# Regrouping the token-wise input products of a hybrid attention block: five groups of 512 columns in place of seven groups of 384 and 256

## The reference, cut to what matters

```python
def hybrid_layer(x, mem, norm_g, w_in, w_out, mem_norm_g, w_mem_kv, qk_g):
    h = rms_norm(x, norm_g)
    proj = jnp.einsum('btd,de->bte', h, w_in)
    ...
    a_q, a_k, a_v, a_g, b_q, b_k, b_v, b_g, m_q, m_g = jnp.split(proj, cuts, axis=-1)
    qa = rope(rms_norm(to_heads(a_q, N_HEADS_MOBA), qk_g[0]))
    ka = rope(rms_norm(to_heads(a_k, N_HEADS_MOBA), qk_g[1]))
    oa = from_heads(moba_attention(qa, ka, to_heads(a_v, N_HEADS_MOBA)))
    qb = rope(rms_norm(to_heads(b_q, N_HEADS_DIL), qk_g[2]))
    kb = rope(rms_norm(to_heads(b_k, N_HEADS_DIL), qk_g[3]))
    ob = from_heads(dilated_attention(qb, kb, to_heads(b_v, N_HEADS_DIL)))
    mkv = jnp.einsum('bmd,de->bme', rms_norm(mem, mem_norm_g), w_mem_kv)
    m_k, m_v = jnp.split(mkv, 2, axis=-1)
    qm = rms_norm(to_heads(m_q, N_HEADS_MEM), qk_g[4])
    km = rms_norm(to_heads(m_k, N_HEADS_MEM), qk_g[5])
    om = from_heads(memory_attention(qm, km, to_heads(m_v, N_HEADS_MEM)))
    y = jnp.concatenate([oa * jax.nn.silu(a_g), ob * jax.nn.silu(b_g), om * jax.nn.silu(m_g)], axis=-1)
    return x + jnp.einsum('bte,ed->btd', y, w_out)
```

## Time and profile before

| | us |
|---|---|
| median of three runs | 1634.05 |
| the three runs | 1631.53, 1634.05, 1634.16 |
| the profiled execution | 1631.64 |
| span of its profile | 1629.8 |
| PE busy | 1576.7 (97%) |
| DVE busy | 921.9 (57%) |
| ACT busy | 755.0 (46%) |

### The profile page before, as it was taken

One profiled execution on the slowest core, in us unless ns is written; L12 is line 12 of the kernel. 1 busy time (PEld: TensorE's weight loads), 2 busy tenths in 40 slices (PEclk: granted clock), 3 DMA queues, 4 the chain that ended last, 5 costly groups with the idle time before them and its releaser, 6 DMA issues.

```text
span 1629.8 us, 22039 instructions
## 1 busy us (share of the span) xinstructions
PE 1576.7 (97%) x8345; PEld 1305.3 (80%) x8345; DVE 921.9 (57%) x1940; ACT 755.0 (46%) x1587; POOL 46.4 (3%) x75
## 2 busy tenths in 40 slices
PE   6999999999998999999999999999999999999999
PEld 6887778788887887877788888899866779987677
DVE  4597546443444479656435335549665564885653
ACT  5443544333333362555323334535565654556662
POOL 0000001000001000000100000100000010000000
PEclk9999999999999999999999999999999999999999
DMA  7232112333332433212232333333211233312121
GB/s 220 88 90 78 52 40 78 91 93 101 90 101 62 121 91 95 61 52 68 65 103 80 103 102 118 93 88 85 60 47 56 66 107 98 98 51 63 40 78 65
DMA packets 80886, 136.07 MB, mean 83 GB/s; under 512 B 8191, under 2 KB 33549, under 8 KB 80781
## 3 DMA queue, kind: packets, MB, share of 16 engines
q1 hardware_dynamic: 77120, 129.22, 27.0%
q10 hardware_dynamic: 3660, 5.44, 1.1%
HBM read 132.55 MB, written 2.10 MB: 83 GB/s over the span
## 4 chain that ended last, share of the span: by engine, by line
PE 86%; DVE 9%; ACT 3%; issue 1%; DMA 0%; ACTq 0%; POOL 0%; DVEq 0%
PE gemm_bank L728 71%; PE aux_bank L854 3%; PE aux_bank L833 3%; PE aux_bank L814 2%; PE aux_bank L798 2%; DVE w_lo L1472 2%; PE aux_bank L783 1%; ACT w_hi L1107 1%; DVE rope L1574 1%; PE aux_bank L700 1%; PE aux_bank L1017 0%; PE aux_bank L842 0%; PE aux_bank L908 0%; DVE q L1535 0%; DVE k L1535 0%
## 5 line engine op out<-in xcount | busy, mean ns | idle before, releaser
L1107 ACT ACTIVATE w_hi<-raw 128x512 fp32r<-128x512 f32 (+3 forms) x524 | 305.2, 587 | 625.5 <-PE gemm_bank L728 624.9
L1472 DVE TENSOR_TENSOR w_lo<-raw,w_hi 128x512 fp32r<-128x512 f32 (+3 forms) x524 | 330.0, 635 | 427.2 <-ACT w_hi L1107 425.5
L728 PE MATMUL gemm_bank<-act_hi,w_hi 128*128 128x512 f32 x768 | 311.4, 405 | 9.4 <-DVE bgT L2085 3.3
L728 PE MATMUL gemm_bank<-act_hi,w_lo 128*128 128x512 f32 x768 | 300.1, 391 | 0.0
L728 PE MATMUL gemm_bank<-act_lo,w_hi 128*128 128x512 f32 x768 | 299.7, 390 | 0.0
L728 PE MATMUL gemm_bank<-w_hi,act_hi 128*128 128x384 f32 (+3 forms) x736 | 265.6, 361 | 1.1 <-DVE qk_c L1512 1.1
L728 PE MATMUL gemm_bank<-w_hi,act_lo 128*128 128x384 f32 (+3 forms) x736 | 256.9, 349 | 0.0
L728 PE MATMUL gemm_bank<-w_lo,act_hi 128*128 128x384 f32 (+3 forms) x736 | 256.7, 349 | 0.0
L728 PEld LDWEIGHTS gemm_bank<-act_hi,w_hi 128*128 128x128 f32 x768 | 144.2, 188 | 47.4 <-issue 15.3
L728 PEld LDWEIGHTS gemm_bank<-act_hi,w_lo 128*128 128x128 f32 x768 | 144.3, 188 | 31.1
L728 PEld LDWEIGHTS gemm_bank<-act_lo,w_hi 128*128 128x128 f32 x768 | 144.6, 188 | 28.6 <-issue 1.0
(11 more groups left out here) (303 smaller groups left out, 2093.9 us busy)
## 6 DMA issues: line engine op xcount, KB each, us to landing
raw<-in_w_in SPq DMA_DIRECT2D x104, 512.0 KB, 3.6
raw<-in_w_in SPq DMA_DIRECT2D x64, 384.0 KB, 3.3
raw<-in_w_out SPq DMA_DIRECT2D x32, 512.0 KB, 3.9
raw<-in_w_branch SPq DMA_DIRECT2D x24, 512.0 KB, 3.8
raw<-in_w_mem_kv SPq DMA_DIRECT2D x8, 512.0 KB, 3.7
raw<-in_w_in SPq DMA_DIRECT2D x16, 256.0 KB, 2.8
raw<-in_w_in SPq DMA_DIRECT2D x8, 416.0 KB, 4.8
x<-in_x SPq DMA_DIRECT2D x4, 512.0 KB, 5.1
```

Of the source, the lines that this page charges most:

```text
L728: last = pe.matmul(o, a, c, start=begin and n == 0, stop=end and n == 2)
L1107: act.activation(w_hi[:, s % RING, 0:n], raw[:, p % RAW, kk % PIECE, 0:n], ACT.Copy)\
L1472: dve.tensor_tensor(w_lo[:, s % RING, 0:n], raw[:, p % RAW, kk % PIECE, 0:n], w_hi[:, s % RING, 0:n].bitcast(F32), ALU.subtract).then_inc( ...
```

## The change

The seven token-wise products of a layer of block 2 are no longer groups of their own. Their 2560 columns stand in one line, aq, ak, bq, bk, av, bv, mq, and are cut every 512 columns: t0 is aq and the first 128 columns of ak, t1 the other 256 of ak and 256 of bq, t2 the last 128 of bq and bk, t3 is av and 128 of bv, t4 the other 256 of bv and mq. t0, t1, t2 are plain, t3 is led (in av's place), t4 is filler (in place of bv and mq). A weight piece of such a group is two DMAs, one for each part, and a bank is evicted in two instructions, all on ACT. The events ahead of the led group move two k-steps later, and scores 3 goes to the start of attention. The heads of a have three pieces for each k-step over t2 and the first three of t3, and those of b begin with k-step 5 of t3.

```diff
+TOKEN_FEATURES = [("aq", 0, WA), ("ak", WA, WA), ("bq", 4 * WA, WB), ("bk", 4 * WA + WB, WB),
+                  ("av", 2 * WA, WA), ("bv", 4 * WA + 2 * WB, WB), ("mq", 4 * WA + 4 * WB, WE)]
+def token_groups():
+    out, at = [[]], 0
+    for what, c0, n in TOKEN_FEATURES:
+        done = 0
+        while done < n:
+            if at == T:
+                out.append([])
+                at = 0
+            m = min(n - done, T - at)
+            out[-1].append((what, done, at, c0 + done, m))
+            at, done = at + m, done + m
+    return out
...
-        two("aq", 0, WA)
-        two("ak", WA, WA)
-        two("bq", 4 * WA, WB)
-        two("bk", 4 * WA + WB, WB)
-        two("av", 2 * WA, WA)
-        two("bv", 4 * WA + 2 * WB, WB)
-        two("mq", 4 * WA + 4 * WB, WE)
+        for tag, segments in TOKENS.items():
+            def tokens(k0, k1, segments=segments, l=l):
+                return [(at, w["w_in_2"][l, k0 * P:k1 * P, c:c + m]) for _, _, at, c, m in segments]
+            add((2, l, tag), tokens, KD, T, 4)
...
-        fill = [((2, l, g), KD) for g in ("bv", "mq", "ag", "bg", "mg")] + [((2, l, "out", 0), EARLY)]
+        fill = [((2, l, g), KD) for g in ("t4", "ag", "bg", "mg")] + [((2, l, "out", 0), EARLY)]
...
-        a.lead = {2: [("turn", 0, 0)], 3: [("low", 0, 0)], 4: [("scores", 0)], 5: [("scores", 2)], 6: [("scores", 3)]}
-        for m in (2, 3):
-            a.begin[0].remove(("scores", m))
+        a.lead = {4: [("turn", 0, 0)], 5: [("low", 0, 0)], 6: [("scores", 0)], 7: [("scores", 2)]}
+        a.begin[0].remove(("scores", 2))
...
-            evict(gi_of(2, l, "aq"), ACT.Copy, lambda b: flat_2("aq")[:, b, :])
-            split.through(gi_of(2, l, "ak"))
+            def evict_tokens(name):
+                gi = gi_of(2, l, name)
+                for b in range(NT):
+                    wait_gemm_full(act, gi, b)
+                    for what, c, at, _, m in TOKENS[name]:
+                        ins = act.activation(flat_2(what)[:, b, c:c + m], gemm_bank[b][:, at:at + m], ACT.Copy)
+                    ins.then_inc(gemm_read[b], 1)
+            for name in ("t0", "t1"):
+                split.through(gi_of(2, l, name))
+                evict_tokens(name)
...
-            gi = gi_of(2, l, "av")
+            gi = gi_of(2, l, "t3")
             for kk in range(KD):
-                for _ in range(2):
-                    next(b_squares, None)
+                if kk > 4:
+                    for _ in range(2):
+                        next(b_squares, None)
                 split.beside(gi, kk)
...
-            evict(gi_of(2, l, "ak"), lambda b: flat_2("ak")[:, b, :])
+            split.through(gi_of(2, l, "t1"))
...
-            alongside(a_heads, [gi_of(2, l, n) for n in ("bq", "bk")], 2)
+            alongside(a_heads, [gi_of(2, l, "t2")], 3, drain=False)
             for kk in range(KD):
                 for event in a.lead.get(kk, []):
                     if event[0] != "turn":
                         begin(a, *event)
-                for _ in range(2):
+                for _ in range(3 if kk < 3 else 0):
+                    next(a_heads, None)
+                for _ in a_heads if kk == 3 else ():
+                    pass
+                for _ in range(2 if kk > 4 else 0):
                     next(b_heads, None)
-                split.beside(gi_of(2, l, "av"), kk)
+                split.beside(gi_of(2, l, "t3"), kk)
```

More of the change, by code:

```diff
@@ L57 @@
 PIECE = 2
+TOKEN_FEATURES = [("aq", 0, WA), ("ak", WA, WA), ("bq", 4 * WA, WB), ("bk", 4 * WA + WB, WB),
[12 more added lines that the diff above has]
+    return out
+TOKENS = {f"t{i}": segments for i, segments in enumerate(token_groups())}
 def constants():
@@ L576, in mode @@
         def mode(self, key):
-            return "tokens" if key[2] in ("vc", "bv", "mq", "out") else "features"
+            return "tokens" if key[2] in ("vc", "out") or key[2] in TOKENS else "features"
         def step_that_ends(self, *key):
@@ L847, in values @@
             if a.block == 2 and g in (0, FIRST_B):
-                wait_gemm_read(pe, gi_of(2, a.l, "bv" if g else "av"))
+                wait_gemm_read(pe, gi_of(2, a.l, "t4" if g else "t3"))
             aux_wait_read(pe, a.key("T", a.steps_of[g * NT + NT - 1][-1]))
@@ L1383, in block_2 @@
         def block_2(l):
-            evict(gi_of(2, l, "aq"), ACT.Copy, lambda b: flat_2("aq")[:, b, :])
-            split.through(gi_of(2, l, "ak"))
+            def evict_tokens(name):
[8 more added lines that the diff above has]
+                evict_tokens(name)
             def kind_tiles(a):
                 return [kinds[a + n][:, t, :, :] for n in ("q", "k") for t in range(NT)]
-            wait_gemm_read(act, gi_of(2, l, "aq"))
-            wait_gemm_read(act, gi_of(2, l, "ak"))
+            wait_gemm_read(act, gi_of(2, l, "t1"))
             for n, _ in enumerate(head_squares(kind_tiles("a"), sq_2)):
[L1393 to L1397, removed]
+                split.beside(gi_of(2, l, "t2"), n // 2)
+            split.through(gi_of(2, l, "t2"))
+            evict_tokens("t2")
+            wait_gemm_read(act, gi_of(2, l, "t2"))
             b_squares = head_squares(kind_tiles("b"), sq_2)
             a = attention_2(l)
-            gi = gi_of(2, l, "av")
+            gi = gi_of(2, l, "t3")
             for kk in range(KD):
-                for _ in range(2):
-                    next(b_squares, None)
+                if kk > 4:
+                    for _ in range(2):
+                        next(b_squares, None)
                 split.beside(gi, kk)
@@ L1410, in block_2 @@
                         exponentials(a, event[1])
-            evict(gi, ACT.Copy, lambda b: flat_2("av")[:, b, :])
+            for event in a.lead[KD - 1]:
+                exponentials(a, event[1])
+            split.through(gi)
+            evict_tokens("t3")
             m_squares = head_squares([mq_tok[:, t, :, :] for t in range(NT)]
                                      + [mkv[:, t, 0, :, :] for t in range(NMEM // P)], sq_2)
-            n_m = a.step_that_ends(2, l, "mq")
+            n_m = a.step_that_ends(2, l, "t4")
             _, hi_at, _ = y2_plan(a)
@@ L2048, in block_2 @@
             dve.wait_ge(causal_loaded, 16)
-            split.through(gi_of(2, l, "aq"))
-            evict(gi_of(2, l, "ak"), lambda b: flat_2("ak")[:, b, :])
+            split.through(gi_of(2, l, "t0"))
+            split.through(gi_of(2, l, "t1"))
             def kind_heads(a, gain):
```

12 lines of the change are left out of this document (6 added, 6 removed).

## The result

The changed kernel takes 1653.43 us (median of four runs, 1651.03 to 1654.15), the kernel before 1634.11 in the same comparison (1631.53 to 1634.71): the ratio is 1.0119, with a 95% interval from 1.0101 to 1.0136, so 19.3 us or 1.2% slower. The forecast was 1649, in a range from 1638 to 1660.

A forecast was written before the change was run, and what follows sets the result against it. PE's own work, plus a few waits for DVE or ACT, was taken as the bound. A layer adds 14.5 and saves 6.45 us, +16.1 for two; from 1632.8 that gave 1649, range 1638 to 1660.

The forecast's parts named there:

- The waits that come: New PE waits for DVE or ACT in block 2, priced place by place: 14.5 us a layer.
- turn 0: PE reaches it after twelve k-steps of t2 and t3, before the heads of a end: 1.0 us a layer (0.3 to 2).
- scores 4: Attention scores waiting for low parts of pair 1, queued on DVE behind two sums: 1.9 us a layer (1.2 to 2.6).
- T(3): Step behind scores 4, waiting for exponentials whose row maxima follow a Newton chain on DVE: 1.5 us a layer (1.0 to 2.0).
- turn 3: Heads of b, only six pieces done ahead of attention, are drained there: the largest wait, 3.9 us a layer (3.3 to 4.4).
- The waits that go: Waits at scores 3, scores 7 and two old borders removed or shortened, with restarts: 3.9 us a layer (3.3 to 3.9).
- PE's saving: In block 2, 192 fewer matmuls a layer at 13.3 ns fixed part each, same columns: 2.55 us saved a layer.
- lesser shifts: Small added waits at scores 11, 19 and 23: 0.6 us a layer (0 to 1.2).
- The clock: Rival: new long waits lower PE's clock, adding 6 to 8 us in all, giving 1656; chance 0.11.
- a granted clock under 0.99: Sign in the changed profile that was to show the lower PE clock at work.
- Late pieces: Rival: narrower weight DMAs come late, 2.72 us for each piece missed, a few a layer giving 1660; chance 0.04.
- The faster rival: DVE and ACT run further ahead, most added waits fall, some −2 us a layer, 1629; chance 0.14.

The follow-up runs named there:

- experiment 6: The kernel of experiment 5 with the filler's banks shared out so four borders lie between steps, and a third piece of the heads of b at steps 2, 7, 9: 1615.52 us.
- experiment 9: The kernel before (seven groups) with low parts ahead of the weight splitting, and filler shared out so mq ends with step 10 and bg with step 28: 1619.01 us.
- experiment 10: The kernel before with each weight piece of its seven token-wise groups loaded by two DMAs instead of one: 1632.63 us.
- experiment 1: The changed kernel with three pieces of the heads of b instead of two at each attention step from step 2 on: 1648.49 us.
- experiment 2: The changed kernel with filler weights of six steps changed so borders ag/bg, bg/mg and mg/out0 lie between two steps: 1647.37 us.
- experiment 4: The kernel before (seven groups) with squares and heads of b begun at k-step 5 of av instead of k-step 0: 1642.05 us.
- experiment 3: The changed kernel with the squares and sums of b one k-step of the led group earlier (from k-step 4): 1640.79 us.
- experiment 5: The kernel of experiment 3 with a pair's low parts on DVE ahead of the splitting of weights of the turn's step: 1633.17 us.

## Why the prediction was right, point by point

**The waits that come** were taken place by place, and the distances from start to start, less columns and 13.3 ns, give them again (layer 0, layer 1; the last row is what the four waits grew by against the kernel before):

| place | forecast | measured |
|---|---|---|
| turn 0 | 1.0 | 1.14, 1.14 |
| turn 1 | 1.2 | 0.96, 0.95 |
| scores 4 | 1.9 | 1.93, 0.94 |
| T(3) | 1.5 | 1.43, 1.44 |
| turn 3 | 3.9 | 3.74, 3.74 |
| border of ag and bg | 2.3 | 2.25, 2.24 |
| border of mg and out0 | 2.1 | 1.98, 1.98 |
| scores 11, 15, 19, 23 | 0.6 | 0.7, 1.2 |

Turn 3 shows how such a term is reckoned. The timeline of layer 0:

```profile
1186.56 0.45 PE L833 MATMUL aux_bank<-k_hi,q_hi 64*128 64x384 f32 x2
...
1187.50 0.56 DVE L1663 CUSTOM_DVE_ANT_0 probs<-aux_bank,mask_square 128x384 f32<-128x384 f32 x1
...
1192.53 0.95 DVE L1611 TENSOR_TENSOR bk<-rope,rope 128x768 f32<-128x768 f32 x1
...
1193.59 1.12 PE L802 MATMUL aux_bank<-ident,bq 128*128 128x128 f32 x4 [3.53 <-DVEq L1616]
```

Scores 10 start at s = 1186.56, the row maximum at s+0.94, the last subtraction ends at s+6.92, the turn starts at s+7.03; forecast were s+0.93, s+6.95 and 0.2 more. Here the mechanism was forecast, and not only the number.

**The waits that go** came to 1.0, 1.13, 1.13 and 0.6, 3.87 a layer for 3.9. The borders that were to keep 0.4 and 1.2 keep 0.50 and 1.20. (The four terms of the text add up to 3.29 and not to 3.35, and a restart cost 0.16 to 0.21 and not 0.13; the two slips nearly cancel.)

**PE's saving** is seen in the matmuls, 384 fewer, whose 512 columns stand 227 ns apart as before. By the earlier trace rows they are worth 5.1 us. All of PE's distances in block 2 add up with it: in the two layers 2.56 and 2.55 less for the matmuls, 10.3 and 9.8 more of waits (idle for over 0.1 us), 1.4 and 3.5 more at low clock, and 0.2 more and 0.4 less of the rest make the 9.25 and 10.40. Experiments 6 and 9 lie 3.5 apart, with 0.7 of waits against the five groups. The Trainium skill (TensorE: Matmul & The Clock Gate, Back-to-back issue gap) has 2.5 ns as the fixed part of an isolated matmul's gap; by an estimate from that page five groups could be worth 1 us here. The measured 3.5 agrees with the rows and not with this estimate, as far as two versions that differ in more than their groups can tell.

**Where the sum was off.** It gave +16.1 and block 2 grew by 19.65. Without the clock it was 14.5: scores 4 were priced with a table load that ACT has in layer 0 only, 1 us too much in layer 1, and most other terms run up to 0.2 high (turn 0 is 0.1 low). In the "lesser shifts" 1.5 at scores 15 were not seen; they were made up for in part by scores 11, which wait less behind the long wait at turn 3 (0.7 and 0.2 less), and by scores 19 (0.2 less). The clock, +5.1, was in the text as a rival with 6 to 8 and a chance of 0.11: it did not stand in the forecast's place but came on top of it. A cost that follows from the forecast's own waits belonged in the sum as a term, not among the rivals. That the time came within 4.4 us of the forecast is thus in part luck: a term that was left out and waits that were priced too high stand against each other.

Two things on the clock were also read wrongly. The low stretch of the earlier trace rows does not follow the border of bg and mg, which PE reaches only at 1248.9; it follows scores 19:

```profile
1229.93 0.50 PE L814 MATMUL aux_bank<-k_hi,q_hi 64*128 64x512 f32 x2 [1.64 <-DVE k_lo L1620]
```

And a granted clock under 0.99 could not have been its sign: 6 to 8 us of 1650 lower the mean by no more than 0.005, and it went from 0.999 to 0.994. The rule of the Trainium skill (TensorE: Matmul & The Clock Gate, What's actually happening), 1.2 GHz after idleness and 2.4 GHz again with activity, agrees with the stretches at both turns 3 (0.55 to 0.60 granted). Layer 0's border of ag and bg, with the same wait of 2.25 as layer 1's, keeps full clock, and no run here shows why.

**What the rivals were worth.** Late pieces: no (experiment 10, and the `w_lo` waits beside it). The faster rival: no, `k_lo` of pair 1, which was to decide, came after PE (1.9 and 0.9 us). The rival of the experiments, that a wait which is taken away comes back at the next place, is half right: experiments 1 and 2 show waits that change places and 4 a wait that covers another, 3 and 5 show waits that go. What the evictions in two pieces, and that of ak on ACT, add to turn 0 (1.14 a layer) was not tested by itself.

## What to carry to other kernels

Fewer and wider groups save a fixed part for each matmul, but they move every border, event and piece of side work that is placed by count: price each of these by what then stands ahead of it on the engine that is waited for. Before work is moved to end a wait, look for idle time of that engine, and look at what is queued behind the place it is moved to: put into an idle stretch most of it was gained, put ahead of the next awaited instruction it was paid back. A long wait covers later ones, which come out when it goes. An instruction that others wait for should not stand behind one that waits itself: that order alone cost the kernel before 7.6 us.

## What the runs showed of the hardware

A wait of 1.6 to 3.7 us on PE is followed in some places by a window of 4 us at a mean granted clock of 0.57 (most of it at 1.2 GHz), worth 1.7 us, and in others, at the same wait, by none; behind turn 3 of layer 0 there were two such windows. The same start of a layer of block 1 ran at 0.57 in one execution and at 1.00 in another. So differences of 2 to 3 us between two profiles of this kernel can be the clock's alone, and a gain has to be counted net of it before it is put down to an edit: of the 4.3 us by which experiment 1 made the two layers shorter 3.4 were clock.
